# Stick-breaking and gated-linear-attention block on one core: plain single-precision products for the first tile of both output projections

## What is computed

```python
h    = rmsnorm(x) ; proj = h @ w_in
o_sb  = stick_breaking(q, k, v)                 # 8 heads of 64
o_gla = rmsnorm(gla_chunked(q, k, v, alpha))    # 4 heads, 64 keys, 128 values
y_sb  = (o_sb  * silu(z_sb))  @ w_o_sb          # 1024x512 @ 512x1024
y_gla = (o_gla * silu(z_gla)) @ w_o_gla         # 1024x512 @ 512x1024
merged = sigmoid(gA) * y_sb + sigmoid(gB) * y_gla
out = rmsnorm(x + merged @ w_out)
```

## Time and profile before

| | us |
|---|---|
| median of 3 runs | 820.55 (820.23 to 822.45) |
| profiled execution, its own time | 820.71 |
| its span, first to last instruction | 818.6 |
| PE busy | 793.8 (97%) |
| DVE busy | 580.9 (71%) |
| ACT busy | 410.5 (50%) |
| POOL busy | 50.6 (6%) |

### The profile page before, as it was taken

One profiled execution on the slowest core, in us unless ns is written; L12 is line 12 of the kernel. 1 busy time (PEld: TensorE's weight loads), 2 busy tenths in 40 slices (PEclk: granted clock), 3 DMA queues, 4 the chain that ended last, 5 costly groups with the idle time before them and its releaser, 6 DMA issues.

```text
span 818.6 us, 11843 instructions
## 1 busy us (share of the span) xinstructions
PE 793.8 (97%) x4441; PEld 664.0 (81%) x4441; DVE 580.9 (71%) x811; ACT 410.5 (50%) x706; POOL 50.6 (6%) x44
## 2 busy tenths in 40 slices
PE   5999999999999999999999999999999999999896
PEld 5778888888888888879889888888888888888685
DVE  6528896989698698946645656665467776778865
ACT  8536675756666465655254153344343333465432
POOL 1630000000000000020000000000000000012500
PEclk9999999999999999999999999999999999999899
DMA  9852011112110220021110001234433344384222
GB/s 321 286 200 52 26 40 40 49 42 60 35 41 26 52 51 26 27 78 53 44 36 26 26 29 52 86 134 138 143 116 104 109 129 128 132 304 175 103 104 102
DMA packets 72483, 76.31 MB, mean 93 GB/s; under 512 B 3804, under 2 KB 57207, under 8 KB 71928
## 3 DMA queue, kind: packets, MB, share of 16 engines
q1 hardware_dynamic: 72386, 75.71, 28.8%
q10 hardware_dynamic: 54, 0.01, 0.0%
HBM read 55.79 MB, written 15.73 MB: 87 GB/s over the span
## 4 chain that ended last, share of the span: by engine, by line
PE 79%; DVE 10%; issue 5%; ACT 4%; POOL 1%; DMA 0%; DVEq 0%; ACTq 0%; POOLq 0%
PE pj L715 22%; PE tr L1019 5%; PE ob L967 5%; PE sc L967 5%; PE pj L859 4%; PE pj L1019 4%; PE ob L1019 4%; DVE surv L1680 4%; PE ob L807 3%; PE sc L1019 3%; PE pj L731 3%; PE tr L817 3%; PE pj L840 3%; PE sc L784 2%; PE tr L1077 2%
## 5 line engine op out<-in xcount | busy, mean ns | idle before, releaser
L715 PE MATMUL pj<-h_hi,w_lo 128*128 128x512 f32 x336 | 134.1, 399 | 0.0
L715 PE MATMUL pj<-h_hi,w_hi 128*128 128x512 f32 x336 | 133.8, 398 | 0.0
L715 PE MATMUL pj<-h_lo,w_hi 128*128 128x512 f32 x336 | 133.6, 398 | 0.0
L1680 DVE TENSOR_TENSOR_SCAN surv<-surv 128x128 f32<-128x128 f32 (+3 forms) x64 | 86.4, 1350 | 19.2 <-ACT beta L1186 18.7
L715 PEld LDWEIGHTS pj<-h_hi,w_lo 128*128 128x128 f32 x336 | 63.5, 189 | 12.1 <-issue 0.5
L715 PEld LDWEIGHTS pj<-h_lo,w_hi 128*128 128x128 f32 x336 | 63.3, 188 | 12.0 <-issue 0.3
L715 PEld LDWEIGHTS pj<-h_hi,w_hi 128*128 128x128 f32 x336 | 63.5, 189 | 11.7 <-issue 0.2
L1227 ACT ACTIVATE wt_hi<-tr 128x512 fp32r<-128x512 f32 (+2 forms) x96 | 43.6, 490 | 43.2 <-PE tr L817 41.7
L1603 DVE TENSOR_TENSOR w_lo<-w_raw,w_hi 128x1024 fp32r<-128x1024 f32 x33 | 40.3, 1221 | 26.7 <-ACT w_hi L1119 26.5
L1725 DVE TENSOR_TENSOR wt_lo<-tr,wt_hi 128x512 fp32r<-128x512 f32 (+2 forms) x96 | 50.0, 548 | 5.3 <-ACT wt_hi L1227 4.8
L1683 DVE TENSOR_TENSOR beta<-beta,surv 128x128 f32<-128x128 f32 (+3 forms) x64 | 48.5, 758 | 2.2
(11 more groups left out here) (400 smaller groups left out, 1932.5 us busy)
## 6 DMA issues: line engine op xcount, KB each, us to landing
w_raw<-in_w_in SPq DMA_DIRECT2D x30, 512.0 KB, 3.6
y_scratch<-y_ring SPq DMA_DIRECT2D x28, 256.0 KB, 2.0
graw<-in_w_in SPq DMA_DIRECT2D x14, 512.0 KB, 4.6
y_back<-y_scratch SPq DMA_DIRECT2D x14, 512.0 KB, 5.1
x_t<-in_x SPq DMA_DIRECT2D x8, 512.0 KB, 6.2
wrow<-in_w_out SPq DMA_DIRECT2D x4, 1024.0 KB, 7.6
w_scratch<-wsum SPq DMA_DIRECT2D x4, 1024.0 KB, 4.7
wout_raw<-in_w_out SPq DMA_DIRECT2D x8, 512.0 KB, 6.9
```

Source lines behind the costliest of these rows:

```text
L715: mm = pe.matmul(pj[bank][:, :], (w_lo if p == 2 else w_hi)[:, slot, k, :], (h_lo if p == 1 else h_hi)[:, k, HALF * h:HALF * h + HALF], st ...
L1680: dve.tensor_tensor_scan(s[:, ::-1], s[:, ::-1], s[:, ::-1], 1.0, ALU.mult, ALU.bypass)\
```

## The change

The first tile is multiplied from `G` and `w_raw` as they are, both plain `F32`: 4 matmul calls for a bank in place of 12, 16 for the tile in place of 48. PE waits once for all 8 low parts of `G` ahead of them. The load that takes the first tile's slot of `w_raw` (number 32) waits in addition until the first tile's four banks are done (`y_ready` 4). The high and low parts of `G` and of the first tile's weights are still made.

```diff
@@ -514,6 +514,8 @@
             def load_y(n):
 
                 sp.wait_ge(lo_done, n - 1)
+                if n == 32:
+                    sp.wait_ge(y_ready, 4)
                 parts = ((0, 0), (0, 1)) if n == 30 else Y_PARTS[n]
@@ -971,10 +973,13 @@
             gate_tile(N4 + 1, (N4 + 1) % 2, 2)
             pe.wait_ge(lo_done, 31)
+            pe.wait_ge(gs_lo, 8)
             for h in range(2):
                 for br in range(2):
-                    pe.wait_ge(gs_lo, 4 * br + 4)
-                    y_products(2 * h + br, 0, br, br, h)
+                    for k in range(4):
+                        mm = pe.matmul(ring4[2 * h + br], w_raw[:, 0, 4 * br + k, :],
+                                       G[:, 4 * br + k, HALF * h:HALF * h + HALF], start=(k == 0), stop=(k == 3))
+                    mm.then_inc(y_ready, 1)
             for n, parts in Y_PARTS.items():
```

## The result

| | before | changed |
|---|---|---|
| median, us | 821.85 (5 runs, 820.23 to 822.55) | 825.08 (5 runs, 824.26 to 826.34) |
| profiled span, us | 818.6 | 823.9 |

The ratio is 1.0045, 95% interval 1.0026 to 1.0063: slower, by 2.1 to 5.2 us. The forecast was 823.8 from a median of 820.55, a step of 3.2 us; the medians lie 3.2 us apart, and the ratio of 1.0045, taken over all runs, is 3.7 us. But the two profiled spans lie 5.3 us apart, and a part of the forecast's working does not hold, as follows.

What follows compares the result with a forecast made beforehand. PE's list was taken to bound the kernel. The first tile's 14.10 us in place of 10.88 gave +3.2 us, waits and weight loads nothing, so 820.55 + 3.2 = 823.8 us, range 822.7 to 825.7.

Steps and rivals of the forecast that it cites:

- PE alone bounds the stage: Around the first tile PE is busy throughout; every nanosecond on its list moves everything behind; the tile costs 10.88 us before.
- A plain call is two matmuls and each column counts twice: First tile: 16 plain calls become 32 matmuls (halves), a half costing what a reduced product of twice the columns costs.
- The size of a half: First tile: a 512-column half takes 0.4407 us, extended from 128 columns; tile 14.10 us against 10.88, +3.2 us.
- The four passes: First tile by the skill's rule that true FP32 takes four array passes: 13.65 us, an estimated +2.8 us.
- Weight loads at nothing: First tile: PE's 32 weight loads, 192 ns each, are overlapped by the halves and cost nothing.
- The wait for all low parts of G: PE's wait ahead of the first tile costs nothing, with 2.5 us to spare.
- the wait of load 32: Load 32, issued only when the first tile is done, is ready 4.5 us before PE needs it; costs nothing.
- Nothing on the path: Behind load 32's wait, SP, ACT and DVE work queued later still meets PE's needs, adding no time.
- One pass in a half: Rival: a 512-column half costs like a reduced product, 0.2267 us; tile 7.25 us, time 816.9 us; chance 0.08.
- Loads laid bare: Rival: each first-tile half also pays its 0.19 us weight load, +6 us more, 829.9 us; chance 0.05.
- Tile 32 late: Rival: load 32 lands only after PE needs it; landing after 16 us would give 8 us waiting, 832 us; chance 0.03.
- It does not do what it says: Rival: plain calls are built as 16 single reduced products, tile 3.63 us, time 813.3 us; chance 0.02.

Runs made afterwards that it cites:

- high parts alone: Changed kernel with the first tile made from high parts only, 16 reduced products, so it computes less: 815.01 us, ratio 0.992 to the kernel before.
- the kernel that used up the slack: Kernel before with load 32 held back until y_ready 7, three banks of load 31 done: 827.25 us, ratio 1.0073.
- 256-column kernel: Changed kernel with each plain call of 512 columns cut into two of 256, 64 halves: 825.19 us, ratio 1.0048 to the kernel before.
- late weight sums: DVE's weight sums moved behind the second PSUM addition in the gate-column stage: on the kernel before 820.64 us, ratio 1.000; on the changed one 823.38, 1.0023.
- repeated kernel before: The kernel before measured and profiled once more, with no edit: 821.25 us, ratio to itself 0.9999.

## Why the prediction was right, and where it was not

- **PE alone bounds the stage: right.** Plain products made twice cost their 13.7 us in the chain, high parts alone gave back 6.4 of 7.25 us.
- **A plain call is two matmuls and each column counts twice: right.** 32 halves in the trace; 0.2159 us at 256 columns and 0.4294 at 512.
- **The size of a half, "0.1206 + 3 x 0.1067 = 0.4407 us": 11 ns too high.** The step that failed carries the fixed part of 14 ns from a half of 128 columns to one of 512. At 256 and 512 columns a half has some 2.5 ns over its columns, while a reduced product has 13.3 ns at either size. Both points that I had measured, 0.1206 and 0.1200, hold their own fixed part, and that they are alike says nothing of the one at 512. The term was 2.86 us and not 3.2, inside the bounds of 2.8 to 4.5. The four passes of the Trainium skill, page "FP8 and Floating Point Precision", section "TensorE Precision Notes", gave an estimate of 13.65 us for the tile; the chain measured 13.74, so the trace agrees, and more closely than with the 14.10 of the rows.
- **Weight loads at nothing: right**, 190 ns under 429.
- **The wait for all low parts of G and the wait of load 32 at nothing: right.** Together they made a ratio of 0.9997; 4.8 us to spare where the forecast had 4.5, and the kernel that used up the slack showed where it ends.
- **"Nothing on the path" behind load 32: right for the output projections, wrong for the program.** I followed the delay to the end of the projections and stopped. The stage after it has 0.7 us to spare in each round between DVE's addition and PE, behind a transfer. With the changed kernel that slack ran out in both of its profiles and cost 2.4 and 1.3 us of the stage; with the kernel before it cost 0 and 0.8. By the medians the change came to 3.2 and 4.1 us in place of 2.9. That the forecast of 3.2 met the first of them is in part luck: two errors of it, 0.3 us too much for the halves and 0.3 to 1.3 us too little for the rest, leaned against each other, and the clock in the last stage moves single runs by 1 to 2 us.
- **One pass in a half: refuted** by the 256-column kernel. **Loads laid bare: refuted** by the chain. **Tile 32 late: did not happen**, and the kernel with load 32 held back shows that a wait there costs half as much again as its idle time, which I had not priced, by the fall of the clock. **It does not do what it says: refuted**, the trace has 32 matmuls of 592 ns.

No version that computes the same beat the kernel before. The late weight sums make the later stage safe against landings of up to at least 6.6 us, but by 1.000 (0.9991 to 1.0009) they gain nothing measurable where the landings are early.

## What to carry to other kernels

Count the matmuls that a plain single-precision call becomes and the columns that each is charged for before trading parts against it: here 16 calls are 32 matmuls at double columns, dearer than 48 reduced ones. A change that only lengthens the bounding engine's list can still lose time at a later place where a transfer, an in-order engine and a bank of PSUM stand in one line; read the slack of the stages behind the change as well. In such a line put the work that must free the bank ahead of the work that waits for memory.

## What had not been expected of the hardware

- A run of plain halves has a smaller fixed part than a run of reduced products: 2.7 ns a matmul (0.4294 us less 0.4267 for 1024 columns at the upper level of 2.4 GHz) against 13.3 (0.2267 less 0.2133 for 512), though both have a weight load of 188 to 190 ns for each.
- After 3.8 us of idle time TensorE's granted clock fell to 0.79 on the mean of 7 us, and 24 matmuls took 7.37 us in place of 5.44. After 1.35 us of idle time in the changed kernel's gate stage it stayed at 1.00. Around the end of the wait for `x_res` it fell in twelve of the thirteen profiles, in one of them with a wait of 3.3 us, and did not fall in the thirteenth, with 3.5 us; from the end of that wait to the end of the span it took 53.5 us without the fall and 54.9 to 56.3 with it.
- A late semaphore can cost time without any matmul shown as idle: in the repeated kernel before the weight loads waited 1.3 us, the matmuls none, and the stage took 0.8 us more.
- The two transfers of 512 KB into `graw` that are issued in the fourth round had both landed after 5.1 us in the kernel before and after 7.0 us in the changed one, whose list of transfers is the same. Where PE depended on such a transfer, the stage took 129.6 us; with the dependence taken out it took 127.2, although the transfer landed after 6.6 us.
